# Linear attention's outputs moved into the latent heads, and the output weight's rounding spread over heads 8 to 10, in a two-layer hybrid attention trunk

## The reference, cut to what matters

```python
q_dec, k_inv = qc * jnp.exp(cum), kc * jnp.exp(-cum)
o_inter = jnp.einsum('bnchk,bnhkv->bnchv', q_dec, s_prev)
a = jnp.einsum('bnihk,bnjhk->bnhij', q_dec, k_inv)
a = jnp.where(mask, a, 0.0)
o_intra = jnp.einsum('bnhij,bnjhv->bnihv', a, vc)
o = rms_norm(o_fwd + jnp.flip(o_bwd, axis=1), norm_w)
y = o.reshape(z.shape) * jax.nn.silu(z)
```

## Time and profile before

| what | value |
|---|---|
| median of 3 runs | 1039.66 us (1039.33 to 1041.62) |
| the profiled execution's own time | 1039.05 us |
| its span, first to last instruction | 1036.9 us |
| mean granted TensorE clock | 0.974 |
| busy, share of the span | PE 93%, PEld 64%, DVE 49%, ACT 41%, POOL 13% |
| layer 0: stage, heads, output | 251 to 304, 304 to 516, 516 to 570 us |
| layer 1: stage, heads, output | 774 to 816, 816 to 980, 980 to 1027 us |

### The profile page before, as it was taken

How to read it: one execution, slowest core, us unless ns; L and a number is a source line. 1 busy time by engine, 2 the same in 40 slices (tenths; PEclk the granted TensorE clock), 3 DMA queues, 4 the chain that set the end, 5 groups by cost and what they waited for, 6 DMA issues and landing times.

```text
span 1036.9 us, 12558 instructions
## 1 busy us (share of the span) xinstructions
PE 960.7 (93%) x4563; PEld 667.0 (64%) x4563; DVE 510.0 (49%) x873; ACT 420.5 (41%) x755; POOL 136.9 (13%) x158
## 2 busy tenths in 40 slices
PE   4899999998999999999899889899998999999896
PEld 3587889886555554555488677688765545445485
DVE  4456443444843544655542654443647444555544
ACT  5435343212115445576901523433321254555802
POOL 1110000002340001000920100000022301000720
PEclk9899999999989999999999899899999899999998
DMA  9640312204001322040043111321322000022022
GB/s 346 240 115 23 82 41 62 62 22 162 1 1 48 116 82 82 1 153 10 17 159 92 62 47 36 81 62 42 102 87 76 1 0 1 1 82 81 1 102 82
DMA packets 67867, 74.12 MB, mean 71 GB/s; under 512 B 6148, under 2 KB 47456, under 8 KB 67680
## 3 DMA queue, kind: packets, MB, share of 16 engines
q1 hardware_dynamic: 61392, 60.17, 18.3%
q0 software_dynamic: 4016, 12.77, 3.4%
q10 hardware_dynamic: 2400, 0.38, 0.2%
HBM read 69.11 MB, written 4.19 MB: 71 GB/s over the span
## 4 chain that ended last, share of the span: by engine, by line
PE 82%; DVE 7%; ACT 5%; issue 4%; POOL 1%; ACTq 1%; DVEq 0%; POOLq 0%
PE pv L1719 10%; PE bank L1506 9%; PE bank L1507 9%; PE bank L1508 8%; PE bank L1770 6%; PE bank L1680 4%; PE bank L1801 3%; PE bank L1802 3%; PE bank L1803 3%; PE bank L1647 2%; PE bank L1627 2%; PE bank L1696 2%; PE bank L1549 2%; PE bank L1550 2%; PE bank L1548 2%
## 5 line engine op out<-in xcount | busy, mean ns | idle before, releaser
L1506 PE MATMUL bank<-hA_parts,W_parts 128*128 128x512 f32 (+1 forms) x496 | 181.3, 365 | 8.6 <-DVE h_low_parts L1037 5.9
L1507 PE MATMUL bank<-hA_parts,W_parts 128*128 128x512 f32 (+1 forms) x496 | 174.7, 352 | 0.0
L908 ACT ACTIVATE hA<-bank 128x512 f32<-128x512 f32 (+1 forms) x168 | 92.5, 561 | 82.2 <-PE bank L1770 56.1
L1313 DVE TENSOR_REDUCE mxp<-bank 128x1 f32<-128x384 f32 x192 | 96.5, 550 | 47.4 <-PE bank L1680 47.1
L1506 PEld LDWEIGHTS bank<-hA_parts,W_parts 128*128 128x128 f32 x496 | 95.3, 192 | 27.8 <-issue 11.1
L1508 PE MATMUL bank<-h_low_parts,W_parts 128*128 128x512 f32 (+1 forms) x310 | 109.2, 352 | 0.0
L1507 PEld LDWEIGHTS bank<-hA_parts,W_parts 128*128 128x128 f32 x496 | 95.3, 192 | 13.5 <-issue 2.2
L1719 PE MATMUL pv<-hA,vg 128*128 128x512 f32 (+1 forms) x168 | 83.1, 576 | 6.8 <-ACT hA L908 6.4
L1719 PE MATMUL pv<-hA,XA 128*128 128x512 f32 (+1 forms) x168 | 81.0, 563 | 2.4 <-ACT hA L908 2.3
L1044 DVE TENSOR_TENSOR W_parts<-W,W_parts 128x1024 fp32r<-128x1024 f32 x44 | 53.5, 1221 | 32.0 <-ACT W_parts L635 31.9
L1331 DVE SCALAR_TENSOR_TENSOR hA<-pv,hA 64x512 f32<-64x512 f32 (+1 forms) x36 | 21.6, 599 | 90.8 <-ACT hA L851 90.6
(11 more groups left out here) (261 smaller groups left out, 1834.1 us busy)
## 6 DMA issues: line engine op xcount, KB each, us to landing
W<-in_w_in SPq DMA_DIRECT2D x39, 512.0 KB, 4.0
W<-in_w_mod SPq DMA_DIRECT2D x8, 2048.0 KB, 8.0
W<-in_w_out SPq DMA_DIRECT2D x4, 2048.0 KB, 7.8
gqk<-in_w_mod SPq DMA_DIRECT2D x2, 1536.0 KB, 9.2
cqkv<-in_w_mod SPq DMA_DIRECT2D x2, 1536.0 KB, 13.7
XA<-in_x SPq DMA_DIRECT2D x4, 512.0 KB, 7.1
XA<-in_x POOLq DMA_DIRECT2D x4, 512.0 KB, 6.7
x_between_layers<-XA POOLq DMA_DIRECT2D x4, 512.0 KB, 2.9
```

Source lines behind the costliest of these rows:

```text
L908: act.activation(prob[slot % 4][:, 0:nq], ps("sc", l, h, q0, kt)[:, 0:nq], ACT.Exp, scale=MLA_SCALE if h < MLA_H else GQA_SCALE)\
L1313: dve.tensor_reduce(mxp[:, t, half:half + 1], ps("mx", l, h, q0, t, half)[:, 0:384], AX, ALU.max).then_inc(*up("part_max", l, h, q0, t, half))
L1506: pe.matmul(p[:, 0:c[1]], high[:, k, :], h_hi[:, k, toks], start=(k == 0), stop=False)
L1507: pe.matmul(p[:, 0:c[1]], low[:, k, :], h_hi[:, k, toks], start=False, stop=False)
```

## The change

- `gla_o`, `gla_t` and `gla_a` move into the units of the latent heads: in head h, `gla_o` of tile h behind unit 0, `gla_t` of tile h-1 behind unit 1, `gla_a` of tile h+1 behind unit 2 (layer 0) or 1 (layer 1). The stage keeps `gla_a` of the first tile, the values and head 0's maxima.
- Both directions share one masked tile: the backward mask loses its diagonal, and GpSimd's `two_diagonals` multiplies the diagonal by 2. `gla_o` has four masked products in place of eight.
- `qbd` is made by GpSimd, not VectorE. The first tile's `qbd` and `Sbd` are made before the last projections. Buffers move accordingly.
- `mla_v` moves from VectorE to ScalarE, ahead of head 0. `o_out` is split (copy behind unit 1, root behind unit 3).
- VectorE's order: the context part of `normalise` stands between the context and the latent maxima; `o_scale` stands before tile 4's.
- In layer 1 `ga2` stands behind `ss1l`, not before `gq1`.
- `w_high` takes one piece of half 0 at eight units of heads 8 to 10, and the whole of half 1 behind the last `y_high`.

```diff
+def seq_of(layer):
+    if layer == 0:
+        return SEQ
+    rest = [item for item in SEQ if item != "ga2"]
+    i = rest.index("ss1l") + 1
+    return rest[:i] + ["ga2"] + rest[i:]
+W_HIGH_AT = [(8, 5), (9, 1), (9, 2), (9, 3), (9, 4), (10, 1), (10, 2), (10, 3)]
...
 # POOL
-                pool.memset(hA[:, 2048:4096], 0.0).then_inc(*up("bd_zero", l))
+                def gla_in(t):
+                    for d in range(2):
+                        if t - 1 in out_tiles(l):
+                            pool.wait_ge(*at("filled", "A", l, t - 1, d))
+                        pool.tensor_tensor(qbd[d], ...).then_inc(*up("qbd", l, t, d))
                     for d in range(2):
                         pool.wait_ge(*at("state", l, d))
                         if t - 1 in out_tiles(l):
...
+                def two_diagonals(t):
+                    pool.wait_ge(*at("A_masked", l, t, 1))
+                    pool.tensor_tensor(Ab[t % 2], Ab[t % 2], twofold..., ALU.mult)\
+                        .then_inc(*up("A_both", l, t))
+                pool.memset(QK[:, 0:1024], 0.0).then_inc(*up("bd_zero", l))
+                pool.wait_ge(*at("filled", "kdT", l, 1, 1))
+                gla_in(out_tiles(l)[0])
...
                 for h in heads[1:MLA_H]:
                     round_k(l, h)
+                    if h < len(out_tiles(l)):
+                        gla_in(out_tiles(l)[h])
+                        two_diagonals(out_tiles(l)[h])
...
 # ACT
-                        c = j - 3 if h == heads[-2] else j + len(todo) - 4 if h == heads[-1] and j else -1
-                        if 0 <= c < KD:
-                            w_high(2 * c // KD, (2 * c % KD, 2 * c % KD + 1))
+                        u = j - len(todo) + TILES
+                        if h in (8, 9, 10) and (h, u) in W_HIGH_AT:
+                            w_high(0, (W_HIGH_AT.index((h, u)),))
...
                 y_high((6, 7))
+                w_high(1, range(KD))
...
 # DVE, head loop
                     if h:
                         normalise(h - 1, *qbs(l)[-1][:2])
+                    tile = tiles[h] if h < len(tiles) else None
+                    if tile is not None:
+                        o_square(tile)
+                    if 0 < h <= len(tiles):
+                        o_gate(tiles[h - 1])
...
-                    if len(qbs(l)) == 2:
-                        normalise(h, *qbs(l)[0][:2])
+                    if h + 1 < len(tiles):
+                        for d in range(2):
+                            a_mask(tiles[h + 1], d)
                     if h + 1 < len(heads):
-                        maxima(h + 1)
+                        maxima(h + 1, tile, h)
...
 # PE
-                    for d in range(2):
-                        pe.wait_ge(*at("A_masked", l, t, d))
-                        for h in range(GLA_H):
+                    pe.wait_ge(*at("A_both", l, t))
+                    for h in range(GLA_H):
...
-                maxes(max_groups(0))
-                for t in tiles:
-                    if t + 1 < TILES:
-                        gla_a(t + 1)
-                    gla_o(t)
-                    if t - 1 in tiles:
-                        gla_t(t - 1)
-                values(range(3))
-                gla_t(TILES - 1)
+                values(range(3))
+                maxes(max_groups(0))
                 values(range(3, TILES))
...
                         flush(2)
+                        if j == 0 and h < len(tiles):
+                            gla_o(tiles[h])
+                        if j == 1 and 0 < h <= len(tiles):
+                            gla_t(tiles[h - 1])
+                        if j == MAX_FROM[l] - 1 and h + 1 < len(tiles):
+                            gla_a(tiles[h + 1])
```

More of the change, by code:

```diff
@@ L273, in build @@
         qr, kr = rounded[0:96, 0, :], rounded[0:96, 1, :]
+        low = h_low_f32[:].rearrange("p k t -> p (k t)")
+        vm = [e.rearrange("p (r c) -> p r c", r=3) for e in
+              [low[:, T + 576 * t:T + 576 * t + 576] for t in range(TILES - 1)] +
+              [tz[:].rearrange("p a b -> p (a b)")[:, 0:576]]]
         con = sb("con", [P, C_END])
@@ L468, in _ @@
                     pool.tensor_copy(w[:, :, 3, :, 1 - h, :], w[:, :, 2, :, h, :]).then_inc(*up("swap_q", l))
-                pool.wait_ge(*at("filled", "F", l, "z7", LAT))
-                pool.memset(hA[:, 2048:4096], 0.0).then_inc(*up("bd_zero", l))
[L472 to L484, removed]
+                def gla_in(t):
+                    for d in range(2):
+                        if t - 1 in out_tiles(l):
+                            pool.wait_ge(*at("filled", "A", l, t - 1, d))
+                        pool.tensor_tensor(qbd[d], qd[d][:, t * P:t * P + P].unsqueeze(1).broadcast_to([P, 4, P]),
+                                           headed.unsqueeze(2).broadcast_to([P, 4, P]), ALU.mult)\
+                            .then_inc(*up("qbd", l, t, d))
                     for d in range(2):
@@ L784, in o_out, with mla_v @@
                         .then_inc(*up("o_rstd", l, t))
+                def mla_v(t):
+                    act.wait_ge(*at("vm_ones", l))
+                    act.wait_ge(*at("filled", "vp", l, t))
+                    src = ps("vp", l, t)[:, 0:384].rearrange("p (r e v) -> p r e v", r=3, e=2)
+                    for e in range(2):
+                        act.activation(vm[t][:, :, 128 * e:128 * e + 64], src[:, :, e, :], ACT.Copy)\
+                            .then_inc(*up("vm", l, t, e))
+                    let_go(("vp", l, t), "vm", l, t, 1)
                 def head_in(h):
@@ L860, in w_high @@
                         if n == 0:
+                            act.wait_ge(*at("filled", "o", l, TILES - 1))
+                            act.wait_ge(*at("y_gla", l, TILES - 1))
+                        else:
                             act.wait_ge(*at("q_both", l, heads[-1]))
@@ L887, in _ @@
                 round_q(0)
-                for t in out_tiles(l):
-                    o_out(t)
+                for t in range(TILES):
+                    mla_v(t)
                 slot = 0
@@ L1302, in maxima @@
                         for t in range(q0 // P, (q0 + nq) // P):
+                            if t == 2 and former is not None and len(qbs(l)) == 2:
+                                normalise(former, *qbs(l)[0][:2])
+                            if t == 4 and tile is not None:
+                                o_scale(tile)
                             if q0 == 0:
```

153 lines of the change are left out of this document (69 added, 84 removed).

## The result

| what | before | after |
|---|---|---|
| median on one chip (4 runs each) | 1040.64 us (1039.33 to 1042.18) | 984.88 us (984.60 to 987.04) |
| the profiled execution's own time, its span | 1039.05, 1036.9 us | 984.78, 982.7 us |
| mean granted TensorE clock | 0.974 | 0.985 |

The ratio is 0.9468 with a 95% interval of 0.9447 to 0.9489. The direction was right. The time is 15.6 us under the predicted 1000.5 and 7.6 under the range's lower end of 992.5: the gain was 54, not 38.5.

A forecast was written before the change was run, and what follows sets the result against it. TensorE was taken as the bound, 82% of the chain. Gains of 31.3 + 5.6 + 4.6, less 3 for new waits, make 38.5 us, from 1039.05 to 1000.5 us; range 992.5 to 1012.

The forecast's parts named there:

- What bounds the kernel: TensorE, 82% of the chain; not full in both layers' stages, layer 1's projections, and heads 10, 11 with the output's start.
- Part 1, what stays in the stage: Stages keep one `gla_a`, values and head 0's maxima at VectorE's pace; layer 0 gives up 39.1 us, layer 1 28.2.
- Part 1, what goes into the heads: Latent heads take `gla_a`, `gla_o`, `gla_t` at unhindered TensorE prices: 21.9 us in layer 0, 14.1 in layer 1.
- New waits, +3: Ten latent heads: waits on GpSimd or for banks cost 3 us; bounds -4 to +12, the low from -0.4 a head.
- Part 2: Layer 1's projections: `ga2` behind `ss1l` removes a 4.2 us wait and slow clock; gain 5.6 us, bounds 0 and 6.1.
- Part 3, `w_out`: Thinner rounding gains 1.4 in layer 0's head 10, 0.7 in head 11, 2.5 at layer 1's output: 4.6, bounds 1 and 7.
- Half 1 at the end: Output of both layers: rounding half 1 of `w_out` behind the last `y_high` costs 0 us, bounds 0 and 5.
- A: Latent heads: VectorE and GpSimd hold each other up, 11 us in place of 3, 1008.5 us; chance 0.15.
- B: Latent heads: `gla_a` waits for `qbd`, slower than before, 1040 us or more; chance 0.03.
- C: Layer 1's projections: `ga2`'s wait only moves to the next norm or weight block, 5.6 us back, 1006 us; chance 0.12.
- D: Output: half 1's rounding does not hide, its reload comes when banks are wanted, +5, 1005.5 us; chance 0.08.
- range: Whole kernel: 992.5 us with no new waits and parts 2 and 3 at their bounds, up to 1012 us.

The follow-up runs named there:

- values_first: Changed kernel with all six value tiles ahead of head 0's maxima in each layer, none behind; 985.59 us, ratio 0.9475 to the kernel before.
- gpsimd_more: Changed kernel with four more GpSimd multiplications by one per tile, 5.1 us a tile; 985.41 us, ratio 0.9473 to the kernel before.
- before_four: Kernel before with only the forward direction's four masked products a tile, the backward ones left out; 1034.90 us, ratio 0.9943.
- ga2_back: Changed kernel with layer 1's `ga2` exponentials put back where the kernel before had them; 989.61 us, ratio 0.9504 to the kernel before.
- before_whigh: Kernel before with the new rounding of `w_out` and its buffers alone, VectorE's order as before; 1032.42 us, ratio 0.9919.
- order_back: Changed kernel with the context part of `normalise` put back before all maxima of the next head; 985.99 us, ratio 0.9466 to the kernel before.
- qbd_vector: Changed kernel with `qbd` made by VectorE again instead of GpSimd; 986.56 us, ratio 0.9484 to the kernel before.
- half1_twice: Changed kernel with each low part of half 1 multiplied by one once more on GpSimd before its release; 997.75 us, ratio 0.9584 to the kernel before.
- whigh_back: Changed kernel with the old schedule and old buffers of `w_out`'s rounding, VectorE's new order kept; 995.35 us, ratio 0.9554 to the kernel before.

## Why the prediction was wrong in size, step by step

**What bounds the kernel** held: TensorE, with four places to gain. All four gave more than I took. Three terms of the sum were mis-sized: `w_out` (4.6 taken, 9.9 measured), head 0's maxima in the stages (4.7 taken in layer 0, 2.4 measured; 3.8 us over both stages), and what goes into the heads with its new waits (39.0 taken, 34.4 measured). These three are 13.7 of the 15.7 us by which the span's gain exceeds the forecast; `ga2` is 0.8 and the rest 1.2.

**Part 1, what stays in the stage.** The step that failed is "these go at VectorE's pace", 4.7 us for ten maxima. TensorE's chain shows them in 2.4, and `values_first` shows that this doesn't hang on the values behind them. The six banks carry the difference; VectorE ends its reading while the heads' scores run. The stages gave 2.1 us more than forecast in layer 0 and 1.7 in layer 1. The prices of `gla_a` and the values were right: 1.72, 3.87 and 4.10 for 1.72 and twice 3.87. The first `gla_a` follows the projections without a wait, as predicted from GpSimd's place in front of them.

**Part 1, what goes into the heads.** Layer 1's four took 3.7, 3.9, 3.7 and 2.2, which is 13.5 against 14.1 (the terms add up to 14.0): the rule that a full head pays in full holds. Layer 0's heads 0, 2 and 4 were not full. They grew by 1.99, 2.92 and 2.92 for 3.7 to 3.9 us of work, since the work went into idle time that was there (1.2, 0.9 and 1.2 us in the kernel before); heads 1 and 3, with 0.1 us idle, grew by 3.67. My -0.4 a head for that stood only in the low bound of the waits.

**New waits, +3.** Nine of the ten heads show none. `gpsimd_more` puts 5.1 us more on GpSimd per tile for nothing, so these waits are far off. In the tenth, head 5 of layer 0, there is one of 2.1 us, where the kernel before had 1.5, and behind it 3.1 us of slow clock: the head grew by 5.75 for 2.2 of work. I had looked for waits of TensorE for `Sbd`, `qbd` and `a_mask`. The one that came was a bystander: head 6's k behind `o_square` on VectorE, because of a copy that ScalarE makes late. By the rule "where the change adds a wait, look what is queued behind it", it could have been found on VectorE's list.

**The sum of part 1** is 36.7 where the forecast with its waits was 28.3: +8.4, of which 3.8 is the stage and 4.6 the heads. The halved products are in it. `before_four` adds what the sum did not need: in the old stage they would have earned 5.4 of their 9.7.

**Part 2** was right: 6.4 in the profiles and 6.7 by `ga2_back`, against 5.6. The 0.5 that I took off for `gk`'s weights is not there.

**Part 3, `w_out`, was taken at 4.6 and gave 9.9.** It is the largest of the mis-sized terms, and off in every piece. I read the cost of the crowded rounding from TensorE's idle time. Head 11's excess was put at 0.7 (2.25 us idle against 1.57); the stretch from its start to the output gave 2.4. Layer 1's output start was put at 2.5, one window's idle time; behind the last head's start 5.3 came off. This is layer 0's stretch from head 11's start to the output, first in the kernel before, then in the changed one:

```profile
502.10:515.70 13.60, 11.63 (x41) 6.03 (x41) 5.21 (x6) 12.47 (x24) 13.04 (x11) 1.00 0.00 1
477.94:489.17 11.23, 10.77 (x41) 6.39 (x41) 4.66 (x7) 9.92 (x18) 0.00 (x0) 1.00 0.00 0
```

Before, it idles 1.97 us, but the same work takes 11.2 in all in the changed kernel, less than the 11.63 that are busy here. So busy time held some waiting; that it is matmuls that had been issued and whose ends the profile models is my inference. The length of the stretch, set against a like one, would have shown it, and the idle time did not. On the other side, layer 1's heads 9 and 10, where a piece a unit is new, pay 0.7 that I had put at nothing. By `before_whigh` the rounding is 7.6 of it. Of the other 2.3, 1.9 is VectorE's order, by the lengths of heads 9 and 10 in `order_back`; what the last 0.4 is stays open.

**Half 1 at the end costs nothing**, as forecast, with 5.0 and 8.2 us to spare.

**The rivals.** A, VectorE and GpSimd holding each other up, has its premise and not its price. In after, `o_square`'s multiply (L1265) has a median of 1.06 us; with `qbd` on VectorE it is 0.43. First the changed kernel, then `qbd_vector`:

```profile
L1265 DVE TENSOR_TENSOR sq<-sq x10: 424/1058/1251, 271.5 to 819.5; 128x256 f32<-128x256 f32 x10
```

```profile
L1274 DVE TENSOR_TENSOR sq<-sq x10: 410/426/1251, 272.9 to 820.4; 128x256 f32<-128x256 f32 x10
```

No head is longer for it. The Trainium skill, page "SBUF — State Buffer", section "Who interferes with whom", which says that the loser waits in full, agrees with these rows in that the single instruction is longer beside GpSimd's work; whether it waits for the whole of GpSimd's instruction they don't show. By the head lengths it changes nothing here. VectorE is busy 14.4 of 26 us of such a head, so I take it that it has room. B and C didn't come: no `gla_a` waits for `qbd` in the changed kernel, and nothing of the size of `ga2`'s wait took its place. D is refuted by `half1_twice` and its room.

The **range** failed at its low end. The case named there, idle time filled in and parts 2 and 3 at their bounds, is worth 7 + 0.5 + 2.4 = 9.9 us by the prediction's own terms and not 8, so the end should have been 990.6 (and A with C adds up to 1014.1, not 1012). That would still have been too high. Part 3's bound of 7 was itself too low, and the stage's 4.7 had no bound of its own.

## What to carry to other kernels

Price a crowded stretch by the length of a like stretch that is not crowded, not by the idle time of the engine in it. When work is moved from a stretch with waits into one that is full, its price is its unhindered time on the bounding engine, and the holes in the receiving stretch come off that; count the holes head by head, since odd and even heads differed by a microsecond. And when an instruction that waits for another engine is put into a third one's list, look for whatever stands behind it there that has nothing to do with the moved work.

## What the runs showed of the hardware that was not expected

The same wait had two prices. Eight profiles hold the wait of 2.1 us in layer 0's head 5. In six of them the head lasts 19.55 to 19.57 us; in two, the changed kernel and `whigh_back`, 22.67 and 22.64. The same 17 us of head 5 in `order_back`, to be read beside after's 380.00:397.00 with its clock of 0.82:

```profile
382.20:399.20 17.00, 14.64 (x60) 8.20 (x59) 9.95 (x20) 10.46 (x21) 0.18 (x1) 1.00 0.00 1
```

Busy time is the same, 14.63 and 14.64, but the clock is 1.00 and more instructions fit (60 for 53). So this wait of 2.1 us was followed by a granted clock of 1.2 GHz instead of 2.4 in two profiles and not in six, at 3.1 us each time. What decides between the two was not tried. It does not explain by itself why the timed runs scatter (984.6 to 987.0): the profiled execution has paid the 3.1 us and is one of the shorter ones, at 984.78. The waits of 5.7 and 3.0 us in `half1_twice` were both followed by a lower clock, at 3.0 and 1.6 us, while the wait of 1.7 us in layer 1's head 5 was followed by one in no profile. A profile's span can be 2 us off for such a reason alone, so what a change is worth is read from the stretches that it touches.
